# A MoBA chain woven through a projection: its load in three pieces, its output transposes moved off it, and its last slots run into the next product

## The chip, the cores and the metric

The kernel runs on one core of a Trainium2 chip. The metric is the device time of one execution in microseconds (us), the median of several runs.

## The reference

A first block and two layers of a second block run over 256 tokens of width 2048, all in float32. The change is in the first block and at one layer boundary of the second. What is computed there, cut to its core:

```
u = rmsnorm(x)
q_a, k_a, v_a, z_a, beta, dec, q_b, k_b, v_b, gate_a, gate_b = split(u @ w_in)
y_a = rmsnorm(delta_rule(conv(q_a, k_a, v_a), beta, dec)) * silu(z_a)      # 8 heads of 128
q_b, k_b = rmsnorm(q_b), rmsnorm(k_b)                                     # per head
y_b = softmax(q_b @ k_b.T * scale + rel_bias, causal) @ v_b               # MoBA: 256 tokens are one block
mix = sigmoid(gate_a) * (y_a @ w_branch_gdn) + sigmoid(gate_b) * (y_b @ w_branch_moba)
h = x + mix @ w_out
...
x2 = layer_norm(ALPHA * x1 + gate * (o @ a_w_out))                        # end of layer 0 of the second block
k, v = split((x2 * (1 + scale) + shift) @ kv_w)                           # first product of the next layer
```

## The kernel before

**Products.** Every large product is a list of bodies and units (`PLAN`). A unit is one 256x512 piece of a weight: SyncE loads it into a ring of `RING` = 4 buffers (`raw`), ScalarE casts it to its high part `w_hi`, VectorE subtracts to get the low part `w_lo` (`split` on both engines), and TensorE multiplies high by high, low by high and high by low: 12 matmuls a unit in `chunk`. The split in slot j is for unit j + 4, and it waits until TensorE has used unit j, so a unit's operands are ready up to three units ahead. Beside it VectorE does one step of a long vector product per slot (`gemv`: a 128x512 piece `gemv_w`, double-buffered, loaded by SyncE in the same queue as the weights). On VectorE and ScalarE a slot is: `between(j)`, then `split`, then (VectorE) `gemv`; on TensorE it is the unit's matmuls, then `due(j)`.

**The chain.** The product "spill" has 8 bodies of 16 units, so 128 slots, numbered here 0 to 127. It computes z, q_b, k_b, v_b and the gates and stores them to DRAM (`spill`). Through the same slots each engine steps a generator `delta_net`, one `next(mixer, None)` per slot, which runs the delta rule and then MoBA attention. The code between two `yield`s is the work of one slot; `rest(n)` is n empty slots; engines meet through semaphores. Slots 0 to 89 are the delta rule. From slot 90 on, before the change:

| | ScalarE | VectorE | TensorE |
|---|---|---|---|
| 90 | load all of `qkv_b` (3 MB), `o_sq` half 0 | | `rel_sum` |
| 91 to 94 | `o_sq` half 1, store `rel_scr`, `root_o`, load `bias_b` (1 MB) | `squares`, `over_root(0)` | |
| 95, 96 | 96: wait for `qkv_b`, `sq_b` half 0 | `gated(0)`, `over_root(1)`, `gated(1)` | |
| 97 | | `squares_b(0)` | transposes of `o_gdn`, pairs 0 and 1 (`ya_ready`) |
| 98 | `ya_high(0)`, `(1)`, `sq_b` half 1 | | pairs 2 and 3 (need `ya_low(0)`, `(1)`) |
| 99 | `ya_high(2)`, `(3)` | `ya_low(0)`, `(1)` | |
| 100 | | `ya_low(2)`, `(3)`, `squares_b(1)` | |
| 101 to 103 | `root_qkb` | norms of q_b and k_b (`qkb_normed`) | 103: first transposes of `qkv_b` |
| 107 on | | | scores of head 0, a head every two slots |

`turn_all` transposes a pair of blocks into one of two PSUM banks; a bank comes free (`turn_free`) when VectorE has taken the low part out of it. The last MoBA step is in slot 125 on TensorE, 126 on ScalarE and 127 on VectorE.

**The next product.** "branch" has 4 bodies of 8 units: four with `ya`, four with `yb`, each with its own gate. After slot 127 ScalarE stores the last spill piece, waits for `yb_done` and for all spill stores, and loads `gates` (two transfers, 4 MB) before its next `split`. `gates` lies over `qkv_b`.

**The layer tail.** At the end of "o2" (and "o3") VectorE's `body` calls `finish` in unit 14 of 16: it drains the last accumulators, adds the residual and takes statistics. Then it does the splits of slots 14 and 15 (they are units 2 and 3 of the next product "v3"), and only then come `bn_aggr`, the root, `normalized`, and the first operand blocks of v3 (`even_block`, `block_low` on VectorE, `odd_block` on ScalarE).

## Time and profile before

| | |
|---|---|
| time, median of 3 runs | 2687.71 us (2687.5 to 2688.08) |
| the profiled execution | 2689.27 us, of which span 2687.5 us |
| TensorE busy | 2616.5 us, 97% of the span |
| VectorE, ScalarE busy | 1820.6 us (68%), 1180.0 us (44%) |
| mean granted TensorE clock | 0.99 |
| bytes moved | 604.93 MB, mean 225 GB/s |

Matmuls are pipelined, so a matmul's row is longer (0.40 us) than the step from one to the next; where TensorE stands still shows as idle time before a row. All times below are microseconds from the start of the span.

### The profile page before, as it was taken

The page shows a single profiled execution, that of the slowest core. Times are in us where ns is not written, and L with a number is a line of the kernel's source. Part 1 is how long each engine was busy: PE and PEld are TensorE (multiplying, and loading weights), DVE is VectorE, ACT ScalarE, POOL GpSimd, SP SyncE. Part 2 cuts the span into 40 slices and gives each one's busy share as a digit, 9 for nine tenths or more (in the row PEclk, how much of TensorE's full clock was granted, in tenths as well). Part 3 has the DMA queues.
Part 4 walks back from the last instruction along what each step waited for, and adds up shares of the span by engine and source line. Part 5 has one row for each costly group of instructions (what it writes and reads, how often), then busy time and mean ns, then how long its engine had stood idle before and what let it go on. Part 6 is the DMA issues. An engine that isn't in the chain of part 4 may idle for free.

```text
span 2687.5 us, 37571 instructions
## 1 busy us (share of the span) xinstructions
PE 2616.5 (97%) x13990; PEld 2207.0 (82%) x13990; DVE 1820.6 (68%) x2371; ACT 1180.0 (44%) x1489; POOL 0.2 (0%) x4
## 2 busy tenths in 40 slices
PE   8999999989999999999999999999999989999997
PEld 8977878767788787888887888799987768999885
DVE  6788667576567777777776667776777665545655
ACT  4464333345434444444443334433386344334642
POOL 0000000000000000000000000000000000000000
PEclk9999999989999999999999999999999999999998
DMA  7677575676757788888887777888845546665463
GB/s 216 193 235 244 182 230 193 213 257 202 255 192 262 252 274 266 272 274 272 271 276 258 246 248 251 277 270 273 264 143 188 182 154 178 184 214 170 126 219 126
DMA packets 313000, 604.93 MB, mean 225 GB/s; under 512 B 26606, under 2 KB 28660, under 8 KB 310684
## 3 DMA queue, kind: packets, MB, share of 16 engines
q1 hardware_dynamic: 301628, 571.92, 66.6%
q10 hardware_dynamic: 11232, 31.10, 3.2%
q8 instruction: 94, 1.54, 0.2%
q14 instruction: 46, 0.38, 0.0%
HBM read 592.31 MB, written 10.62 MB: 224 GB/s over the span
## 4 chain that ended last, share of the span: by engine, by line
PE 90%; DVE 4%; DMA 2%; issue 2%; ACT 2%; DVEq 0%; ACTq 0%; SPq 0%
PE bank L613 21%; PE bank L615 21%; PE bank L614 21%; PE bank L636 6%; PE bank L638 6%; PE bank L637 6%; PE bank L733 2%; PE bank L575 2%; DMA gemv_w<-in_w_mod 1%; ACT w_hi L1215 1%; DVE w_lo L1808 1%; DVE gemv_acc L1833 1%; PE bank L1052 1%; DMA raw<-in_w_branch_gdn 0%; PE bank L941 0%
## 5 line engine op out<-in xcount | busy, mean ns | idle before, releaser
L1808 DVE TENSOR_TENSOR w_lo<-raw,w_hi 128x1024 fp32r<-128x1024 f32 x820 | 1001.7, 1224 | 795.0 <-ACT w_hi L1215 793.4
L1215 ACT CAST w_hi<-raw 128x1024 fp32r<-128x1024 f32 x820 | 860.2, 1050 | 1387.2 <-PE bank L615 1045.8
L613 PE MATMUL bank<-w_hi,u_hi 128*128 128x512 f32 x1216 | 494.8, 407 | 2.1 <-DVE u_lo L1869 2.1
L614 PE MATMUL bank<-w_lo,u_hi 128*128 128x512 f32 x1216 | 484.6, 398 | 0.0
L615 PE MATMUL bank<-w_hi,u_lo 128*128 128x512 f32 x1216 | 484.5, 398 | 0.0
L1833 DVE SCALAR_TENSOR_TENSOR gemv_acc<-gemv_w,small,gemv_acc 128x512 f32<-128x512 f32 x480 | 358.4, 747 | 21.6 <-DMA gemv_w<-in_w_mod 16.1
L613 PE MATMUL bank<-w_hi,s_hi 128*128 128x512 f32 x768 | 310.6, 404 | 1.2 <-DVE w_lo L1808 1.1
L615 PE MATMUL bank<-w_hi,s_lo 128*128 128x512 f32 x768 | 304.3, 396 | 0.0
L614 PE MATMUL bank<-w_lo,s_hi 128*128 128x512 f32 x768 | 304.1, 396 | 0.0
L636 PE MATMUL bank<-s_hi,w_hi 128*128 128x256 f32 x1024 | 289.5, 283 | 0.0
L637 PE MATMUL bank<-s_lo,w_hi 128*128 128x256 f32 x1024 | 288.3, 282 | 0.0
L638 PE MATMUL bank<-s_hi,w_lo 128*128 128x256 f32 x1024 | 288.3, 282 | 0.0
L613 PEld LDWEIGHTS bank<-w_hi,u_hi 128*128 128x128 f32 x1216 | 231.2, 190 | 62.0 <-issue 8.2
L615 PEld LDWEIGHTS bank<-w_hi,u_lo 128*128 128x128 f32 x1216 | 230.9, 190 | 56.5
L614 PEld LDWEIGHTS bank<-w_lo,u_hi 128*128 128x128 f32 x1216 | 231.5, 190 | 51.9
L637 PEld LDWEIGHTS bank<-s_lo,w_hi 128*128 128x128 f32 x1024 | 193.3, 189 | 0.3
L638 PEld LDWEIGHTS bank<-s_hi,w_lo 128*128 128x128 f32 x1024 | 193.2, 189 | 0.0
L636 PEld LDWEIGHTS bank<-s_hi,w_hi 128*128 128x128 f32 x1024 | 192.0, 187 | 0.7 <-issue 0.5
L615 PEld LDWEIGHTS bank<-w_hi,s_lo 128*128 128x128 f32 x768 | 144.7, 188 | 35.2
L613 PEld LDWEIGHTS bank<-w_hi,s_hi 128*128 128x128 f32 x768 | 144.7, 188 | 34.7 <-DVE w_lo L1808 1.5
L614 PEld LDWEIGHTS bank<-w_lo,s_hi 128*128 128x128 f32 x768 | 144.9, 189 | 32.6
L613 PE MATMUL bank<-w_hi,hid_hi 128*128 128x512 f32 x352 | 140.0, 398 | 0.0
(355 smaller groups left out, 3012.1 us busy)
## 6 DMA issues: line engine op xcount, KB each, us to landing
gemv_w<-in_w_mod SPq DMA_DIRECT2D x384, 256.0 KB, 3.1
raw<-in_w_in SPq DMA_DIRECT2D x176, 512.0 KB, 4.3
raw<-in_a_w_in SPq DMA_DIRECT2D x128, 512.0 KB, 4.5
raw<-in_w_ffn_gate SPq DMA_DIRECT2D x88, 512.0 KB, 4.6
raw<-in_w_ffn_up SPq DMA_DIRECT2D x88, 512.0 KB, 4.4
raw<-in_w_ffn_down SPq DMA_DIRECT2D x88, 512.0 KB, 4.1
gemv_w<-in_kv_w_mod SPq DMA_DIRECT2D x128, 256.0 KB, 3.6
raw<-in_kv_w SPq DMA_DIRECT2D x64, 512.0 KB, 3.7
```

The lines of the kernel that those rows point to most:

```text
L575: ins = pe.transpose(b[:, f * T + th * P:f * T + (th + 1) * P], src(f, th), ident)
L613: pe.matmul(o, xh, w_hi[:, s, t], start=(k == 0), stop=False)
L614: pe.matmul(o, xh, w_lo[:, s, t], start=False, stop=False)
L615: ins = pe.matmul(o, xl, w_hi[:, s, t], start=False, stop=(k == 2 * units - 1))
L636: pe.matmul(o, wh, hi[:, k], start=(k == 0 and f % 2 == 0), stop=False)
L637: pe.matmul(o, wh, lo[:, k], start=False, stop=False)
L638: ins = pe.matmul(o, wl, hi[:, k], start=False, stop=(k == 2 * half - 1 and f % 2 == 1))
L733: ins = pe.matmul(dst[:, h * P:(h + 1) * P], lhs[:, th, h], rhs[:, th, h], start=True, stop=True)
L1052: ins = pe.matmul(b[:, P:3 * P], queries_of[p][:, a, P:T], k_t[:, a, 0:T], start=True, stop=not mask)
L1215: act.copy(w_hi[:, s], raw[:, s]).then_inc(hi_done, 1)
L1808: dve.tensor_tensor(w_lo[:, s], raw[:, s], w_hi[:, s].bitcast(F32), ALU.subtract).then_inc(lo_done, 1)
L1833: dve.scalar_tensor_tensor(out=gemv_acc[:], in0=w_k, scalar=c_k, in1=gemv_acc[:], op0=ALU.mult, op1=ALU.add).then_inc(gemv_step, 1)
```

## The change

The chain is moved by some slots, its load is cut in three, and its last steps run on into the first body of "branch":

- **The load.** `qkv_b` comes in three transfers of 1 MB: q and k of half 0 in slot 90, of half 1 in slot 92 (ahead of the store of `rel_scr`), all of v in slot 99. The squares wait for the first two, `moba_out(0)` for the third.
- **The output transposes.** TensorE transposes `o_gdn` pairs 0 and 1 in slot 100 (before: 97) and 2 and 3 in slot 102 (before: 98). `ya_high` is in ScalarE's slots 101 and 103 (before: 98, 99), `ya_low` in VectorE's 101 and 104 (before: 99, 100). `squares_b(1)` is in slot 99 (before: 100), behind `sq_b` half 1 in ScalarE's slot 98. `root_qkb` stays in slot 101, the norms in 102 and 103.
- **Two slots later.** The transposes of `qkv_b` begin in TensorE's slot 105 (before: 103), the scores of head 0 in 109 (before: 107). The last steps are in slots 127 (TensorE), 128 (ScalarE) and 129 (VectorE), so the two latter in "branch".
- **The gates.** `gates` lies over `u_hi` and `u_lo`, which are dead after "spill", and ScalarE loads them in slot 1 of "branch", after one more split and without waiting for `yb_done`. `o_gdn`, `ya_lo`, `bias_b`, `mix_hi`, `mix_lo` and two of the delta rule's buffers move to other places.
- **The layer tail.** `finish` ends the body; the splits of slots 14 and 15 come behind `even_block(0)` and `block_low(0)`.

```diff
@@ placement @@
-        o_gdn = slot("o_gdn", 13, [P, H1, HALVES, DH])
+        o_gdn = slot("o_gdn", 10, [P, H1, HALVES, DH])
...
-        gates = slot("gates", 0, [P, HALVES, 2 * D])
-        mix_hi = slot("mix_hi", 4, [P, KD, T], F32R)
-        mix_lo = slot("mix_lo", 10, [P, KD, T], F32R)
+        gates = slot("gates", 3, [P, HALVES, 2 * D])
+        mix_hi = slot("mix_hi", 11, [P, KD, T], F32R)
+        mix_lo = slot("mix_lo", 13, [P, KD, T], F32R)
@@ TensorE: delta_net @@
-                yield from rest(7)
+                yield from rest(10)
                 n0 = products["branch"].ahead0
                 pe.wait_ge(signal("ya_ready"), HALVES)
                 for q in range(H1 // 2):
                     turn_all(n0 + q, 1, lambda f, th: o_gdn[:, 2 * q + f, th])
-                    if q % 2:
-                        yield
-                yield from rest(4)
+                    if q == 1:
+                        yield from rest(2)
+                yield from rest(3)
@@ ScalarE: delta_net @@
+                def qkvb_load(th, blocks):
+
+                    n = DH * blocks.start
+                    src = halves(spill[:, SPILL_QKV + n:SPILL_QKV + DH * blocks.stop])
+                    act.dma_start(qkv_b[:, th, blocks].rearrange("p h b c -> p h (b c)"), src[:, th]).then_inc(signal("qkvb_in"), 16)
+
+                first, values = slice(0, 2 * H1), slice(2 * H1, 3 * H1)
...
-                act.dma_start(qkv_b[:].rearrange("p h b c -> p h (b c)"), halves(spill[:, SPILL_QKV:SPILL_GATES])).then_inc(
-                    signal("qkvb_in"), 16)
+                qkvb_load(slice(0, 1), first)
...
+                qkvb_load(slice(1, 2), first)
                 act.wait_ge(signal("rel_ready"), 2)
                 act.dma_start(rel_scr, rel_rows[0:H1, :]).then_inc(signal("rel_out"), 16)
...
-                act.wait_ge(signal("qkvb_in"), 16)
+                act.wait_ge(signal("qkvb_in"), 32)
...
+                qkvb_load(slice(0, HALVES), values)
@@ ScalarE: behind "spill" @@
-            act.wait_ge(signal("yb_done"), H1)
-            act.wait_ge(signal("spilledA"), 16 * products["spill"].bodies)
-            act.wait_ge(signal("spilledB"), 16 * products["spill"].bodies)
-            for x in range(2):
-                act.dma_start(gates[:, :, x * D:(x + 1) * D], halves(spill[:, SPILL_GATES + x * D:SPILL_GATES + (x + 1) * D])).then_inc(
-                    signal("gates_in" + "AB"[x]), 16)
+            def first_branch(j):
+                if j == 1:
+                    act.wait_ge(signal("spilledA"), 16 * products["spill"].bodies)
+                    act.wait_ge(signal("spilledB"), 16 * products["spill"].bodies)
+                    for x in range(2):
+                        first = SPILL_GATES + x * D
+                        act.dma_start(gates[:, :, x * D:(x + 1) * D], halves(spill[:, first:first + D])).then_inc(
+                            signal("gates_in" + "AB"[x]), 16)
+                next(mixer, None)
...
@@ VectorE: body @@
-                    ending = finish and j == pr.units - 2
-                    if ending:
-                        gemv(pr, i, j)
+                    if finish and j == pr.units - 2:
                         finish()
+                        return
@@ VectorE: behind layer_tail("o2", ...) @@
             even_block(0)
+            split(o2, o2.bodies - 1, o2.units - 2)
             block_low(0)
+            split(o2, o2.bodies - 1, o2.units - 1)
```

Three places show how the order of instructions moves. The first is VectorE from slot 97 on; `small<-sq_b` is `squares_b`, and a `w_lo` row with the `gemv_acc` row behind it is the split and the vector step of one slot. Before:

```order
L2054 TENSOR_REDUCE small<-sq_b 128x16
L1808 TENSOR_TENSOR w_lo<-raw,w_hi 128x1024
L1833 SCALAR_TENSOR_TENSOR gemv_acc<-gemv_w,small,gemv_acc 128x512
L1808 TENSOR_TENSOR w_lo<-raw,w_hi 128x1024
L1833 SCALAR_TENSOR_TENSOR gemv_acc<-gemv_w,small,gemv_acc 128x512
L1865 TENSOR_TENSOR ya_lo<-bank,ya_hi 128x512 x2
L1808 TENSOR_TENSOR w_lo<-raw,w_hi 128x1024
L1833 SCALAR_TENSOR_TENSOR gemv_acc<-gemv_w,small,gemv_acc 128x512
L1865 TENSOR_TENSOR ya_lo<-bank,ya_hi 128x512 x2
L2054 TENSOR_REDUCE small<-sq_b 128x16
```

The same place in the changed kernel:

```order
L2071 TENSOR_REDUCE small<-sq_b 128x16
L1827 TENSOR_TENSOR w_lo<-raw,w_hi 128x1024
L1852 SCALAR_TENSOR_TENSOR gemv_acc<-gemv_w,small,gemv_acc 128x512
L1827 TENSOR_TENSOR w_lo<-raw,w_hi 128x1024
L1852 SCALAR_TENSOR_TENSOR gemv_acc<-gemv_w,small,gemv_acc 128x512
L1882 TENSOR_TENSOR ya_lo<-bank,ya_hi 128x512 x2
L1827 TENSOR_TENSOR w_lo<-raw,w_hi 128x1024
L1852 SCALAR_TENSOR_TENSOR gemv_acc<-gemv_w,small,gemv_acc 128x512
L2102 RECIPROCAL small<-small 128x32
L2105 TENSOR_TENSOR qkv_b<-qkv_b,small 128x2048
```

The second `squares_b` has moved one slot ahead of where it was, the first two `ya_low` two slots back; the other two now stand behind both norms (`qkv_b<-qkv_b,small`).

The second place is ScalarE where "spill" ends and "branch" begins: `stage<-bank` and `spill<-stage` are the last spill piece. Before, and then changed:

```order
L1463 CAST yb_hi<-bank 128x256
L1215 CAST w_hi<-raw 128x1024 x2
L1345 ACT_TABLE_LOAD
L1345 ACTIVATE stage<-bank 128x512 x2
L1347 DMA spill<-stage 128x2x512
L1540 DMA gates<-spill 128x2x2048 x2
L1215 CAST w_hi<-raw 128x1024 x8
```

```order
L1473 COPY probs_t<-bank 128x384
L1219 CAST w_hi<-raw 128x1024
L1349 ACT_TABLE_LOAD
L1349 ACTIVATE stage<-bank 128x512 x2
L1351 DMA spill<-stage 128x2x512
L1477 CAST yb_hi<-bank 128x256
L1219 CAST w_hi<-raw 128x1024
L1554 DMA gates<-spill 128x2x2048 x2
L1219 CAST w_hi<-raw 128x1024 x7
```

One cast of "branch" and the last `yb_hi` now stand between the last store and the load of the gates.

The third place is VectorE at the end of "o2", from the last statistics; `xs<-xs,small` is `normalized`, `stage<-bank,modc` is `even_block`, `s_lo` is `block_low`. Before, and then changed:

```order
L2443 BN_STATS small<-xs 128x6 x2
L1808 TENSOR_TENSOR w_lo<-raw,w_hi 128x1024 x2
L2474 BN_AGGR small<-small 128x2 x2
L2483 RECIPROCAL small<-small 128x2
L2498 TENSOR_SCALAR xs<-xs,small 128x512 x4
L2373 TENSOR_SCALAR stage<-bank,modc 128x256 x2
L2380 TENSOR_TENSOR s_lo<-stage,s_hi 128x512
L2373 TENSOR_SCALAR stage<-bank,modc 128x256 x2
L2380 TENSOR_TENSOR s_lo<-stage,s_hi 128x512
```

```order
L2464 BN_STATS small<-xs 128x6 x2
L2495 BN_AGGR small<-small 128x2 x2
L2504 RECIPROCAL small<-small 128x2
L2519 TENSOR_SCALAR xs<-xs,small 128x512 x4
L2394 TENSOR_SCALAR stage<-bank,modc 128x256 x2
L1827 TENSOR_TENSOR w_lo<-raw,w_hi 128x1024
L2401 TENSOR_TENSOR s_lo<-stage,s_hi 128x512
L1827 TENSOR_TENSOR w_lo<-raw,w_hi 128x1024
L2394 TENSOR_SCALAR stage<-bank,modc 128x256 x2
```

The two splits that stood ahead of `BN_AGGR` are now one ahead of the first `block_low` and one behind it.

## Rows read from the trace of the kernel before

**Rows 1.** The waits of TensorE, 540 to 740: total, times, longest.

```profile
PE bank L575 <- DVE o_gdn L2049: 7.6, 1, 7.6
PE bank L575 <- DVE qkv_b L2090: 5.0, 1, 5.0
PE bank L575 <- DVE ya_lo L1865: 3.7, 1, 3.7
PE bank L613 <- DVE w_lo L1808: 3.0, 2, 1.7
```

**Rows 2.** TensorE in time, 567 to 616: start, duration, instruction, idle before it.

```profile
575.07 1.97 PE L575 MATMUL bank<-keep,o_gdn 128*128 128x128 f32 x8 [7.57 <-DVE o_gdn L2049]
576.68 0.78 PE L613 MATMUL bank<-w_hi,u_hi 128*128 128x512 f32 x1
...
580.07 0.40 PE L615 MATMUL bank<-w_hi,u_lo 128*128 128x512 f32 x1
...
584.88 1.97 PE L575 MATMUL bank<-keep,o_gdn 128*128 128x128 f32 x8 [3.71 <-DVE ya_lo L1865]
...
607.87 1.97 PE L575 MATMUL bank<-keep,qkv_b 128*128 128x128 f32 x8 [4.98 <-DVE qkv_b L2090]
609.49 0.78 PE L613 MATMUL bank<-w_hi,u_hi 128*128 128x512 f32 x1
...
614.18 0.39 PE L615 MATMUL bank<-w_hi,u_lo 128*128 128x512 f32 x1
614.41 1.04 PE L575 MATMUL bank<-keep,qkv_b 128*128 128x128 f32 x8
615.20 0.48 PE L613 MATMUL bank<-w_hi,u_hi 128*128 128x512 f32 x1
```

**Rows 3.** Windows: length, busy PE, PEld, DVE, ACT, POOL, PEclk, DMA share, GB/s.

```profile
544.00:570.00 26.00, 23.50 (x100) 17.99 (x98) 17.14 (x20) 15.97 (x16) 0.00 (x0) 0.99 0.97 341
570.00:610.00 40.00, 26.24 (x99) 21.16 (x100) 30.81 (x31) 16.87 (x21) 0.00 (x0) 0.76 0.58 188
717.30:730.50 13.20, 11.48 (x49) 8.95 (x49) 5.85 (x7) 3.47 (x4) 0.00 (x0) 1.00 1.00 394
```

**Rows 4.** VectorE by line, 544 to 610: busy, mean ns, idle before.

```profile
L1808 DVE TENSOR_TENSOR w_lo<-raw,w_hi 128x1024 fp32r<-128x1024 f32 x15 | 18.3, 1221 | 12.2 <-ACT w_hi L1215 12.1
L1833 DVE SCALAR_TENSOR_TENSOR gemv_acc<-gemv_w,small,gemv_acc 128x512 f32<-128x512 f32 x14 | 10.5, 748 | 6.6 <-DMA gemv_w<-in_w_mod 6.6
L2054 DVE TENSOR_REDUCE small<-sq_b 128x16 f32<-128x2048 f32 x2 | 4.6, 2280 | 0.0
```

**Rows 5.** VectorE in time, slots 96 to 103.

```profile
573.79 1.22 DVE L2049 TENSOR_TENSOR o_gdn<-o_gdn,z_sb 128x1024 f32<-128x1024 f32 x1
...
584.15 1.28 DVE L1865 TENSOR_TENSOR ya_lo<-bank,ya_hi 128x512 fp32r<-128x512 f32 x2
...
605.53 2.29 DVE L2090 TENSOR_TENSOR qkv_b<-qkv_b,small 128x2048 f32<-128x2048 f32 x1
```

**Rows 6.** Transfers issued 540 to 620: size, time to landing.

```profile
gemv_w<-in_w_mod SPq DMA_DIRECT2D x17, 256.0 KB, 3.1
qkv_b<-spill ACTq DMA_DIRECT2D x1, 3072.0 KB, 13.5
bias_b<-rel_scr ACTq DMA_DIRECT2D x1, 1024.0 KB, 8.5
```

**Rows 7.** ScalarE in time where "branch" begins.

```profile
714.79 3.89 ACT L1215 CAST w_hi<-raw 128x1024 fp32r<-128x1024 f32 x4 [6.50 <-issue]
...
728.14 2.23 ACT L1215 CAST w_hi<-raw 128x1024 fp32r<-128x1024 f32 x2 [9.46 <-DMA raw<-in_w_branch_gdn]
```

**Rows 8.** VectorE in time at the end of "o2".

```profile
2154.95 2.35 DVE L1808 TENSOR_TENSOR w_lo<-raw,w_hi 128x1024 fp32r<-128x1024 f32 x2
...
2162.93 0.69 DVE L2380 TENSOR_TENSOR s_lo<-stage,s_hi 128x512 fp32r<-128x512 f32 x1 [1.42 <-ACT s_hi L1619]
```

**Rows 9.** TensorE in time at the end of "o2".

```profile
2159.39 0.88 PE L575 MATMUL bank<-keep,xs 128*128 128x128 f32 x3 [8.21 <-issue]
```

More of the change, by code:

```diff
@@ L193, in block_kernel @@
         ya_hi = slot("ya_hi", 7, [P, H1, T], F32R)
[L194 removed]
+        ya_lo = slot("ya_lo", 10, [P, H1, T], F32R)
         qkv_b = slot("qkv_b", 0, [P, HALVES, 3 * H1, DH])
@@ L198, in block_kernel @@
         qk_t = slot("qk_t", 8, [P, 2 * H1, T])
-        bias_b = slot("bias_b", 10, [P, H1, T])
+        bias_b = slot("bias_b", 13, [P, H1, T])
         rel_rows = slot("rel_rows", 11, [P, 512])
@@ L951, in _ @@
                 plain_body("spill", i, u_hi, u_lo, due)
-            for _ in mixer:
-                pass
             pr = products["branch"]
@@ L962, in due @@
                 def due(j):
-                    if j == 1 and not (isinstance(i, int) and i == 0):
+                    if isinstance(i, int) and i == 0:
+                        next(mixer, None)
+                    elif j == 1:
                         turn_mixed(i - 1)
@@ L967, in branch_body @@
                 if isinstance(i, int) and i == 0:
+                    for _ in mixer:
+                        pass
                     pe.wait_ge(signal("yb_done"), H1)
@@ L1408, in delta_net @@
                 yield from rest(2)
-                act.wait_ge(signal("qkvb_in"), 16)
+                act.wait_ge(signal("qkvb_in"), 32)
                 act.activation(sq_b[:], qkv_b[:, 0, 0:2 * H1], ACT.Square).then_inc(signal("qkb_sq"), 1)
+                yield from rest(2)
+                act.wait_ge(signal("qkb_ss"), 1)
+                act.activation(sq_b[:], qkv_b[:, 1, 0:2 * H1], ACT.Square).then_inc(signal("qkb_sq"), 1)
+                yield
+                qkvb_load(slice(0, HALVES), values)
                 yield from rest(2)
@@ L1545, in mixed_high @@
                     his_of_stage(products["branch"], i, 0, mix_hi)
-            body("branch", 0, nothing)
+            body("branch", 0, nothing, first_branch)
             with act.Fori(1, pr.bodies) as i:
@@ L2078, in delta_net @@
                 yield from rest(2)
+                squares_b(1)
+                yield from rest(2)
                 ya_low(0)
@@ L2081, in delta_net @@
                 yield
-                ya_low(2)
-                ya_low(3)
-                squares_b(1)
-                yield from rest(2)
                 dve.wait_ge(signal("root_qkb"), 1)
@@ L2092, in delta_net @@
                     yield
-                yield from rest(4)
+                ya_low(2)
+                ya_low(3)
+                yield from rest(6)
                 for at_ in range(1, B_LAST + 7):
@@ L2266, in _, with first_branch @@
                 body("spill", i, nothing, between)
-            for _ in mixer:
-                pass
             pr = products["branch"]
+            def first_branch(j):
+                next(mixer, None)
+                if j == 4:
+                    for _ in mixer:
+                        pass
             def branch_drain(pr, i, x):
@@ L2285, in mixed_low @@
                     los_of_stage(products["branch"], i, 0, mix_lo, mix_hi)
-            body("branch", 0, branch_drain)
+            body("branch", 0, branch_drain, first_branch)
             with dve.Fori(1, pr.bodies - 1) as i:
```

33 lines of the change are left out of this document (17 added, 16 removed).

## Prediction

> **What bounds the kernel now.** TensorE is busy 97% of the span, so a change pays only where TensorE stands still. The view of who waited for whom, cut to TensorE and to the stretch of the change, comes first [rows 1]: three single waits of its transposes, 7.6, 5.0 and 3.7 us, all for VectorE, and two waits of matmuls for `w_lo`, 3.0 us together, the longer 1.7. The timeline of TensorE places the first three [rows 2]: A at 575.07 (slot 97, for `ya_ready`), B at 584.88 (slot 98, for the bank that `ya_low(0)` frees), C at 607.87 (slot 103, for the norms). The reader is to see there also what follows each: the 8 transposes of A take 576.68 - 575.07 = 1.61 us, the same 8 at 614.41 take 0.79. The windows [rows 3] say why: the granted clock is a mean of 0.76 over 570 to 610, after 0.99 before, so TensorE runs part of it at the lower of its two levels. Last comes VectorE in the same stretch [rows 4, 5]: it is late because it is loaded and because its vector step waits 6.6 us for `gemv_w`, while the transfers run at a share of 0.97 [rows 3], with 3 MB of `qkv_b` and 1 MB of `bias_b` among them [rows 6].
>
> **What the three waits cost.** Idle: 7.57 + 3.71 + 4.98 = 16.3 us [rows 2]. Slow clock after A: 1.61 - 0.79 = 0.8 on the transposes, and the 8 matmuls from 576.68 to 580.07 take 3.39 instead of 8 x 0.235 = 1.88 (0.235 is the step at full clock; one shows from 614.18 to 614.41), 1.5 more: 2.3. B's transposes have the same row of 1.97 as A's, so B gets 2.3 too. After C, 1.62 - 0.79 = 0.8, and 11 matmuls from 609.49 to 614.18 take 4.69 instead of 2.6: 2.9. Together 7.5. The whole is 16.3 + 7.5 = 23.8 us.
>
> **What is left of it.** A: `gated(1)` ended at 575.01 [rows 5], but now TensorE wants it three slots later, after unit 100: 3 x 2.82 = 8.5 us of cover (12 matmuls of 0.235 are 2.82) against 7.57. Even with all of VectorE's old lag it is hidden; if the cover were gone it would cost the 7.57 and the clock. B was built in: bank 0 was wanted straight after slot 98, and `ya_low(0)` stood in VectorE's slot 99, behind a cast and a split. Now it stands in slot 101 and is wanted after unit 102. Is it in time? In the trace of before `gated(1)` ends 7.57 after unit 97, and 6.6 of these are VectorE's waits for `gemv_w` [rows 4]; without them it would be 1.0. From there to the end of `ya_low(0)` VectorE has 5 splits and 5 vector steps (5 x (1.22 + 0.75) = 9.9), two `squares_b` (2 x 2.28 = 4.6) and half a `ya_low` row (0.64) [rows 4, 5], and about 1.5 of waiting, since `sq_b` is one buffer: ScalarE's second square waits for the first sum, and the cast stands behind it. That is 16.6, or 15.6 with neighbouring rows overlapping by some 0.08 each. TensorE takes 5 x 2.82 plus 2 x 0.79 for transposes = 15.7. So `ya_low(0)` is late by 1.0 + 15.6 to 16.6 - 15.7 = 0.9 to 1.9 (I take 1.0, since neighbouring rows do overlap), plus what is left of the `gemv_w` waits. C: the norms and the second pair of `ya_low` come in slots 102 to 104 (2 x 2.29 + 1.28 + 3 splits and steps, 5.9, = 11.8), wanted after unit 105 (3 x 2.82 + 2 x 0.79 = 10.0, counted from the transposes of slot 102): near 1 us of wait for the bank of `ya_low(2)`, since VectorE is nearer its limit than TensorE here.
>
> **The load in pieces.** Nothing shows this load cut, so its effect on `gemv_w` is bounded from both sides. Below: none of the 6.6 us is left, since `gemv_w` is ahead by about one slot and lands in 3.1 when undisturbed [rows 6]. Above: all 6.6. Before slot 97 the bytes beside the weights fall from 4 to 3 MB (v waits until slot 99), which by proportion leaves 5.0; but the old 3 MB stood in one block of 13.5 us, and now 1 MB stands alone, two slots pass, and the next comes. I take 2.5. A rule speaks against the change here. The Trainium skill, "DMA: Bandwidth & Descriptors", section "Issuing engines are not separate DMA queues", says that transfers issued by SP and ACT run on the same 16 engines and interleave whoever started them, so cutting a transfer moves its bytes and removes none; by it all 6.6 us would stay and the time be that of the first rival below, 2671.7, against 2665.3 by the value taken. No row of this trace shows the cut load.
>
> The new waits are then 1.0 + 2.5 at slot 102 and 1.0 at slot 105: **4.5 us** (ends: 0 and 1.9 + 6.6 + 1.0 + 2.3 of clock = 11.8). The chain gives 23.8 - 4.5 = **19.3 us**. The attention slots themselves are only shifted by two; their small waits stay.
>
> **The start of "branch".** Before, ScalarE stood from the last store to its landing and then did four casts in a row from 714.79 [rows 7]; the first of them fed the first `yb` unit, which TensorE awaited for 3.0 - 1.7 = 1.3 us [rows 1]. One cast is now ahead of that wait: 1.3 gained. The next wait, 1.7, is behind the gates: transfers at a share of 1.00 and 394 GB/s [rows 3], ScalarE 9.46 us without a weight [rows 7]. One weight load is now issued ahead of the gates, the rest still queue with them: 0 to 1.7 gained, I take 0.7. The last chain steps on ScalarE and VectorE (slots 128, 129) are hidden under four `ya` units, 11.3 us; without that cover they cost a slot each. Sum **2.0**. The new places of the buffers cost nothing: the same instructions run on the same shapes.
>
> **The layer tail.** Two splits, 2.35 us, leave the path from the statistics to the first transposes of v3, where TensorE stands 8.21 us [rows 8, 9]. The first goes into the 1.42 us that VectorE waited ahead of `block_low(0)` [rows 8] and is free; the second delays `even_block(2)` by 1.2 and what hangs on it. Gain 2.35 - 1.2 = **1.1** (0 to 2.35). At "o3" no split stood there, so nothing.
>
> **Sum.** 19.3 + 2.0 + 1.1 = 22.4. The profiled execution took 2689.27 (span 2687.5), 1.56 above the median of the runs: 2689.3 - 22.4 = 2666.9, and 2687.7 - 22.4 = **2665.3** as a median.
>
> **Rivals.**
> 1. *The lag stays.* The pieces disturb `gemv_w` as the whole did, VectorE is 1.0 + 6.6 = 7.6 late at slot 102, a wait of that length brings the slow clock, 2.3, and 1.0 follows. Waits 10.9, chain gain 12.9, total 16.0: 2671.7. For it: the DMA share of 0.97. Against: a megabyte less in that stretch.
> 2. *All hidden.* No new waits, 1.7 all gone, the tail gives 2.35: 23.8 + 3.0 + 2.35 = 29.2: 2658.5.
> 3. *The change doesn't do what it says.* VectorE is the bound, and TensorE waits as long, only elsewhere: it ends the norms when it did. Then only "branch" and the tail pay: 3.1, so 2684.6, no change that can be told. Against: VectorE was idle 9.2 us of 570 to 610 [rows 3], mostly for casts that themselves stood behind TensorE's waits.
> 4. *The other side.* TensorE's waits were when the transfers caught up; without them the ring of weights starves. The 17 slots from 544 to 614 need 17 x 0.786 MB of weights and vectors (768 KB each) plus 5.2 MB: 18.6 MB. At the 341 GB/s of 544 to 570 [rows 3] that is 54 us, as long as TensorE needs without any wait, against 70 us now. It costs more than the change brings only below 18.6 / 70 = 266 GB/s. If the rate under mixed queues fell to 225, the mean of the kernel (in the table of the profile), it is 83 us, 13 more: 13 - 3 = 10 slower, 2698.
>
> **Chances.** Forecast 0.60 (2661 to 2669), rival 1 0.22, rival 2 0.10, rival 3 0.05, rival 4 0.03. The range takes in rivals 1 and 2 and the ends of the new waits: 2657 to 2675. What a measurement can tell from no change is about 0.2%, 5.4 us: faster 0.92, same 0.05, slower 0.03.
>
> **What would show it.** In the profile after: no wait of TensorE on `o_gdn` at slot 100; one of about 3.5 us on `ya_low(0)` at slot 102; about 1 at the first transposes of `qkv_b`; the granted clock near 1 over the stretch; VectorE's wait for `gemv_w` at 2 to 3 us instead of 6.6; the first `w_lo` wait of "branch" gone; 5.9 instead of 8.2 us ahead of v3's transposes, about 1 of it given back in v3's first units. The prediction is wrong if the wait at slot 102 is over 7, if matmuls begin to wait for `w_lo` between slots 97 and 107, or if the gates push a longer wait into the second body of "branch".

## The result and the profile after

| | before | after |
|---|---|---|
| median | 2687.61 us (2686.59 to 2689.44, 6 runs) | 2669.45 us (2666.77 to 2672.71, 6 runs) |
| profiled execution | 2689.27 us, span 2687.5 | 2669.09 us, span 2667.3 |

The ratio is 0.9932, 95% interval [0.9921, 0.9942]: 18.2 us faster by the medians, 20.2 by the two profiled executions. The forecast was 2665.3 (22.4 us gained), the range 2657 to 2675.

First the view of who waited for whom, TensorE, 540 to 740, of the changed kernel (the answer to [rows 1]):

```profile
PE bank L575 <- DVE ya_lo L1882: 4.8, 2, 4.1
PE bank L575 <- DVE stage L2301: 2.1, 1, 2.1
```

The wait for `o_gdn` and the one for the norms are gone, and so are both for `w_lo`. Of 19.3 us in these rows before, 6.9 are left. 2.1 of them are a wait on `stage` (the product with the gates), which before was 0.7 and is not in the rows shown. TensorE in time (start, duration, instruction, idle before it), for [rows 2]:

```profile
575.37 1.04 PE L575 MATMUL bank<-keep,o_gdn 128*128 128x128 f32 x8
...
586.67 1.97 PE L575 MATMUL bank<-keep,o_gdn 128*128 128x128 f32 x8 [4.15 <-DVE ya_lo L1882]
588.29 0.78 PE L613 MATMUL bank<-w_hi,u_hi 128*128 128x512 f32 x1
588.86 0.63 PE L614 MATMUL bank<-w_lo,u_hi 128*128 128x512 f32 x1
589.29 0.46 PE L615 MATMUL bank<-w_hi,u_lo 128*128 128x512 f32 x1
589.59 0.39 PE L613 MATMUL bank<-w_hi,u_hi 128*128 128x512 f32 x1
...
598.14 1.16 PE L575 MATMUL bank<-keep,qkv_b 128*128 128x128 f32 x8 [0.66 <-DVE ya_lo L1882]
```

The first pair of output transposes (slot 100) finds its data and runs at full clock: 1.04 us. The second (slot 102) waits 4.15 us for the bank, and behind the wait comes the low clock again: 1.97 for the same work, and some 0.6 us more until the matmuls are back at 0.39. The windows (columns as in [rows 3]) say the same of the whole stretch; the last is the branch product up to `mix_hi`:

```profile
544.00:570.00 26.00, 26.00 (x112) 20.33 (x111) 21.12 (x24) 16.76 (x17) 0.00 (x0) 1.00 0.95 329
570.00:610.00 40.00, 35.19 (x169) 28.24 (x168) 34.49 (x35) 22.88 (x29) 0.00 (x0) 0.96 0.85 285
686.50:781.60 95.10, 92.97 (x412) 74.79 (x411) 56.82 (x62) 38.26 (x42) 0.00 (x0) 1.00 0.65 225
```

Over 570 to 610 the granted clock is 0.96 instead of 0.76, TensorE is busy 35 us instead of 26, and the transfers, which stood at 188 GB/s, run at 285. VectorE is now busy for 34.5 of 40 us. Its waits for `gemv_w` (by line, 544 to 610, as in [rows 4]) and the transfers issued (as in [rows 6]):

```profile
L1852 DVE SCALAR_TENSOR_TENSOR gemv_acc<-gemv_w,small,gemv_acc 128x512 f32<-128x512 f32 x18 | 13.5, 748 | 3.1 <-DMA gemv_w<-in_w_mod 3.0
```

```profile
gemv_w<-in_w_mod SPq DMA_DIRECT2D x22, 256.0 KB, 3.5
qkv_b<-spill ACTq DMA_DIRECT2D x3, 1024.0 KB, 7.7
bias_b<-rel_scr ACTq DMA_DIRECT2D x1, 1024.0 KB, 10.6
```

**Where the 20.2 us came from.** Three instructions of TensorE mark the stretches in every kernel: the `rel_sum` product of the chain, the first matmul with `ya_hi`, and the first with `mix_hi`. Before, they start at 547.03, 704.58 and 801.55; after, at 546.58, 686.50 and 781.54. The chain gave 157.55 - 139.92 = 17.6 us, the branch product 96.97 - 95.04 = 1.9. With 0.45 won ahead of the change, that is 20.0 of 20.2. The layer tail gave the rest:

```profile
2137.24 1.94 PE L575 MATMUL bank<-keep,xs 128*128 128x128 f32 x8 [6.07 <-issue]
2139.51 1.94 PE L575 MATMUL bank<-keep,xs 128*128 128x128 f32 x8 [0.33 <-DVE stage L2394]
...
2146.41 1.03 PE L575 MATMUL bank<-keep,xs 128*128 128x128 f32 x8
```

The wait ahead of v3's transposes fell from 8.21 [rows 9] to 6.07. But unit 0 of v3 and what hangs on it then took longer, and by the transposes ahead of unit 1 only 0.2 us of it is left in this execution. Other executions of the same instructions keep more (experiment 4).

### The profile page after: what moved, and what is told of

Its sections match the earlier page's. It is cut to its first block, busy times and chain, and to the rows that moved or that the text cites. A ratio compares the mean times of both kernels' runs of the same rounds, so it can differ in the third digit from the quotient of the medians.

```text
span 2667.3 us, 37574 instructions
## 1 busy us (share of the span) xinstructions
PE 2611.7 (98%) x13990; PEld 2203.6 (83%) x13990; DVE 1820.8 (68%) x2371; ACT 1179.5 (44%) x1489; POOL 0.2 (0%) x4
## 4 chain that ended last, share of the span: by engine, by line
PE 91%; DVE 4%; issue 2%; ACT 2%; DMA 2%; DVEq 0%; ACTq 0%; SPq 0%
PE bank L613 21%; PE bank L615 21%; PE bank L614 21%; PE bank L636 6%; PE bank L638 6%; PE bank L637 6%; PE bank L733 2%; PE bank L575 1%; DVE w_lo L1827 1%; ACT w_hi L1219 1%; DVE gemv_acc L1852 1%; DMA gemv_w<-in_w_mod 1%; PE bank L1056 1%; DMA raw<-in_w_branch_gdn 0%; PE bank L943 0%
```

## Experiments

The runs of one kernel scatter by 2 to 5 us around its median, and several questions here are of 1 us. So each kernel was timed in 5 runs (`pieces_only` in 11) beside the kernel before, and its profiled execution read by the same three marks. "Chain" is `rel_sum` to `ya_hi`, "branch" `ya_hi` to `mix_hi`; slot 102 and 105 are the waits ahead of the second output transposes and of the first of `qkv_b` (in turn_later slot 103 and 105, in turn_shift 103 and 106, in the kernels with the order before 97, 98 and 103).

| kernel | median (before beside it) | ratio | chain | branch | waits of the transposes |
|---|---|---|---|---|---|
| before | 2687.61 | | 157.55 | 96.97 | 7.57, 3.71, 4.98 |
| changed | 2669.45 (2687.61) | 0.9932 [0.9921, 0.9942] | 139.92 | 95.04 | 4.15, 0.66 |
| one_load | 2669.97 (2686.04) | 0.9941 [0.9927, 0.9954] | 142.31 | 93.96 | 3.71, 0.24 |
| pieces_only | 2683.18 (2686.04) | 0.9990 [0.9981, 0.9999] | 153.18 | 97.34 | 3.92, 3.71, 4.97 |
| branch_undone | 2668.66 (2686.04) | 0.9935 [0.9921, 0.9948] | 140.23 | 94.19 | 3.73, 0 |
| tail_undone | 2668.38 (2686.04) | 0.9933 [0.9919, 0.9946] | 140.55 | 96.51 | 3.72, 0 |
| second_sq | 2666.72 (2687.12) | 0.9930 [0.9916, 0.9944] | 139.07 | 96.34 | 3.19, 0.35 |
| turn_later | 2669.25 (2687.12) | 0.9941 [0.9927, 0.9954] | 139.94 | 94.55 | 0, 4.60 |
| turn_shift | 2671.18 (2687.12) | 0.9942 [0.9929, 0.9956] | 142.75 | 95.38 | 1.21, 1.78 |
| warm_tail | 2666.45 (2687.12) | 0.9929 [0.9915, 0.9942] | 140.21 | 94.55 | 3.71, 0 |
| gates_split | 2666.47 (2687.02) | 0.9922 [0.9908, 0.9935] | 139.28 | 93.35 | 3.54, 0.51 |
| bias_late | 2666.68 (2687.02) | 0.9924 [0.9910, 0.9937] | 137.75 | 94.60 | 2.06, 1.78 |
| best3 | 2664.05 (2687.02) | 0.9915 [0.9901, 0.9929] | 138.93 | 93.64 | 3.12, 0.50 |
| best4 | 2663.91 (2687.02) | 0.9913 [0.9899, 0.9927] | 138.30 | 93.24 | 2.62, 0.24 |

How far to trust one execution can be read there too: five kernels have the changed chain untouched (changed, branch_undone, tail_undone, warm_tail, gates_split), and their chains lie between 139.3 and 140.6. Seven have its branch product untouched (changed, one_load, tail_undone, second_sq, turn_later, warm_tail, bias_late): 94.0 to 96.5, mean 95.1. A single execution inside these bands shows no difference.

What makes these bands can be read too. In every kernel with the order of the changed one whose clock stays at 1.00 there, the branch stretch is 92.9 plus TensorE's waits in it: 95.04 with 2.13 of them, 96.34 with 3.49 (second_sq), 93.96 with 1.10 (one_load). In tail_undone (96.51) the clock was at 0.50 from 718.3 to 721.7 besides, and so it was in pieces_only (97.34) from 717.1 to 720.5. The profiled execution of pieces_only is its slowest of 11, 3.9 us above their median.

### 1 and 2. All but the load, and the load alone

`one_load` is the changed kernel with the whole 3 MB issued where the first piece stood:

```diff
-                    pe.wait_ge(signal("qkvb_in"), 3 * 16)
+                    pe.wait_ge(signal("qkvb_in"), 16)
...
-                qkvb_load(slice(0, 1), first)
+                act.dma_start(qkv_b[:].rearrange("p h b c -> p h (b c)"), halves(spill[:, SPILL_QKV:SPILL_GATES])).then_inc(
+                    signal("qkvb_in"), 16)
...
-                qkvb_load(slice(1, 2), first)
...
-                act.wait_ge(signal("qkvb_in"), 32)
+                act.wait_ge(signal("qkvb_in"), 16)
...
-                qkvb_load(slice(0, HALVES), values)
```

> The changed kernel with one load of 3 MB at slot 90 in place of three pieces; everything else as changed. If the large load is what made VectorE wait for gemv_w (my step 2), the waits of gemv between slots 92 and 97 go back from 3.3 to about 6 us, gated(1) ends 3 us later against the rel_sum product, and the transposes of o_gdn at slot 100 wait 1 to 3 us, with the one at slot 102 as long or longer: 2 to 4 us slower than the changed kernel, near 2672. Rival (the pieces do nothing, the other transfers of that stretch are what VectorE waits for): gemv waits stay within 1 us of 3.3, time within 1 us of 2669.

`pieces_only` is the kernel before with these edits the other way round and nothing else.

> The kernel before with only the load cut in three pieces; transposes where they were. My step 2 says that VectorE is 2.5 to 3.3 us earlier at gated(1), and the wait of the transposes at slot 97 falls from 7.57 to 4.3 to 5; the waits at slots 98 and 103 hang on ScalarE and VectorE inside the chain and keep most of their 3.71 and 4.98: 2684 to 2685, a sixth of the whole gain. Rival (the three waits share one cause, the load): all three shrink and the time falls by 8 us or more, to 2680 or below.

VectorE by line, 544 to 610, in one_load and then in pieces_only:

```profile
L1851 DVE SCALAR_TENSOR_TENSOR gemv_acc<-gemv_w,small,gemv_acc 128x512 f32<-128x512 f32 x17 | 12.7, 745 | 6.1 <-DMA gemv_w<-in_w_mod 6.1
```

```profile
L1843 DVE SCALAR_TENSOR_TENSOR gemv_acc<-gemv_w,small,gemv_acc 128x512 f32<-128x512 f32 x15 | 11.2, 747 | 2.9 <-DMA gemv_w<-in_w_mod 2.9
```

The wait for `gemv_w` follows the shape of the load in both orders: 6.6 and 6.1 with one block, 2.9 and 3.1 with pieces, and 1.9 to 4.9 in all twelve executions with pieces. The first rival of the prediction is out. The pieces are smaller, further apart, and the last one is later; which of the three does it was not tested apart. VectorE's lag follows: `gated(1)` starts 26.8 and 26.3 us after `rel_sum` with the block, 23.1 and 23.5 with pieces. In one_load TensorE doesn't wait at slot 100 either, against what was expected; the lag shows as 2.3 us of waits for `w_lo` ahead of it, and the chain is 2.4 us longer, outside the band. The times of one_load and the changed kernel alone can't be told apart. In pieces_only only the wait at slot 97 shrinks, from 7.57 to 3.92:

```profile
PE bank L575 <- DVE qkv_b L2100: 5.0, 1, 5.0
PE bank L575 <- DVE o_gdn L2059: 3.9, 1, 3.9
PE bank L575 <- DVE ya_lo L1875: 3.7, 1, 3.7
```

The others hang on the order inside the chain, as expected. So the pieces are worth 2.4 us (behind the moved transposes) to 4.4 us (in front of them) of chain, 2.9 by the medians; the moves of transposes, squares and norms are worth the other 13 to 15.

### 3. The start of the branch product as before

Chain drained ahead of the branch product on all three engines, gates loaded only after `yb_done`; here ScalarE's part:

```diff
-            def first_branch(j):
-                if j == 1:
...
-            body("branch", 0, nothing, first_branch)
+            for _ in mixer:
+                pass
+            act.wait_ge(signal("yb_done"), H1)
...
+            body("branch", 0, nothing)
...
```

> The changed kernel with the branch product started as before: the chain drained ahead of it on all three engines, the gates loaded only after yb_done. My step 3 prices that at 2.0 us: the stretch from the first matmul with ya_hi to the first with mix_hi goes from 95.0 back to about 97.0, and the waits at its start (1.3 for the first w_lo, 0.7 more) come back: 2671.5. Rival (the wait of 2.13 us on the stage that now stands in body 1 shows that the work is only moved): within 0.5 us of the changed kernel.

The stretch did not go back to 97: it took 94.2, inside the band of the changed one. The waits were 0.5 (`w_lo`) and 0.6 (`stage`), where the changed kernel has one of 2.1. Running on into the next product is worth nothing that shows here. What TensorE waits for in this place begins in ScalarE's row of transfers. In the changed kernel:

```profile
689.02 0.37 ACTq L1351 DMA_DIRECT2D spill<-stage  x1
689.42 0.37 ACT L1477 CAST yb_hi<-bank 128x256 fp32r<-128x256 f32 x1 [0.44 <-ACT stage L1349]
689.69 1.06 ACT L1219 CAST w_hi<-raw 128x1024 fp32r<-128x1024 f32 x1
694.99 0.89 ACTq L1554 DMA_DIRECT2D gates<-spill  x2
```

and of VectorE there:

```profile
702.57 1.29 DVE L2296 TENSOR_TENSOR stage<-bank,gates 128x512 f32<-128x512 f32 x2 [2.02 <-DMA gates<-spill]
```

ScalarE stands from 690.75 to 694.99 until the last store has landed; the gates leave 5.97 us after it was issued. Their first half, the one that VectorE needs, lands 7.5 us later, the second 13.9, and VectorE waits 2.0. From the issue of the store to that of the gates, 3.95 to 5.97 us pass from execution to execution (before 5.48, branch_undone 3.95).

An early store does not help by itself. In one_load, turn_later, warm_tail, bias_late and tail_undone the gates leave 2 us earlier against the first `ya_hi` matmul than in the changed kernel, 6.5 for 8.5, and the first half lands no earlier: 15.7 to 16.9 for 16.0. In branch_undone the gates also leave at 6.5, but the first half lands at 13.8, after 7.4 us instead of 9.3 to 10.3. There no cast stands ahead of them. With the new order the cast frees a buffer, and one 512 KB weight load goes out at 5.7, ahead of the gates; the changed kernel's gates, which left 2.8 us behind that load and not 0.7 to 1.8, took 7.5 again. That this load is what delays the gates is argued from these times, not shown by a run of its own. So the order seems to have two effects here: the wait for `w_lo` of 0.5 goes, and the one on `stage` grows from 0.6 to between 1.1 and 3.5.

### 4. The layer tail as before

The two last splits of o2 go back ahead of the layer norm.

```diff
-            split(o2, o2.bodies - 1, o2.units - 2)
             block_low(0)
-            split(o2, o2.bodies - 1, o2.units - 1)
...
```

> The changed kernel with the end of the attention layer as before (both last splits of o2 ahead of the layer norm). By my step (1.1 us net) the first unit of the second v3 body would come 1.1 us later. By the rival read from the trace of the changed kernel (the 2.1 us won ahead of v3's transposes are lost again because TensorE keeps its lower clock to the end of the first v3 unit): transposes of xs 2.1 us later, but the transposes of unit 1 only 0 to 0.4 us later, and the first unit takes 2.9 us again instead of 4.8. In the whole time no more than 0.4 us, below what the timing can tell.

From VectorE's first row behind o2 (`stage<-bank,gate_bc`; 2151.22 before, 2131.21 changed, 2132.95 here), TensorE's transposes of `xs` start 8.17, 6.03 and 8.16 us later, those ahead of unit 1 15.39, 15.20 and 15.38 later. In these profiles the edit wins 2.1 us and keeps 0.2. The windows from the first transposes to those ahead of unit 1 show why; the kernel before, then the changed one:

```profile
2159.39:2166.60 7.21, 6.75 (x28) 5.34 (x29) 5.48 (x11) 4.05 (x8) 0.00 (x0) 0.70 0.18 67
```

```profile
2137.24:2146.40 9.16, 8.70 (x28) 6.82 (x29) 7.79 (x13) 4.21 (x8) 0.00 (x0) 0.53 0.40 114
```

The same 28 matmul rows took 7.2 us at a mean clock of 0.70 and 9.2 at 0.53: TensorE began earlier and ran almost all of it at the lower level.

But the 0.2 is of these executions. Three kernels have the tail as before and eight the changed one, with nothing added to it. Microseconds behind VectorE's first row behind o2:

| tail | kernel | clock back at 1.00 | transposes ahead of unit 1 |
|---|---|---|---|
| as before | before, tail_undone, pieces_only | 12.4, 12.1, 11.9 | 15.39, 15.38, 15.37 |
| changed | bias_late, branch_undone | 11.5, 11.5 | 13.86, 13.87 |
| changed | second_sq, turn_later | 12.3, 12.6 | 14.15, 14.26 |
| changed | one_load, changed, turn_shift, gates_split | 14.6, 14.7, 14.7, 14.9 | 15.16, 15.20, 15.23, 15.27 |

The first transposes come at 6.0 in all eight, so that 2.1 us are always won; what is left of them goes with the moment at which the clock comes back. In four executions it is 0.1 to 0.2 us, in four 1.1 to 1.5, and 0.75 on the mean. The window of bias_late beside the two above (7.84 us at a mean clock of 0.65):

```profile
2135.87:2143.71 7.84, 7.38 (x28) 5.60 (x28) 7.24 (x13) 3.58 (x7) 0.00 (x0) 0.65 0.38 96
```

### 5. A buffer of its own for the second squares

```diff
-                act.wait_ge(signal("qkb_ss"), 1)
-                act.activation(sq_b[:], qkv_b[:, 1, 0:2 * H1], ACT.Square).then_inc(signal("qkb_sq"), 1)
+                act.activation(sq_b1[:], qkv_b[:, 1, 0:2 * H1], ACT.Square).then_inc(signal("qkb_sq"), 1)
...
-                    dve.tensor_reduce(sm(MX + th * 2 * H1, 2 * H1), sq_b[:], AX.X, ALU.add).then_inc(signal("qkb_ss"), 1)
+                    dve.tensor_reduce(sm(MX + th * 2 * H1, 2 * H1), (sq_b, sq_b1)[th][:], AX.X, ALU.add).then_inc(signal("qkb_ss"), 1)
```

> The changed kernel with a buffer of its own for the squares of the second token half (over the dead o_sq), so that ScalarE no longer waits 4.70 us for VectorE's sum of the first half. Theory (VectorE's own queue sets the 4.15 us wait at slot 102; from gated(1) to ya_low(0) it is idle only 1.12 + 0.34 us, and the 1.12 is ScalarE's late cast): the 1.12 goes, the wait at slot 102 falls to about 3.0, 1 us faster than the changed kernel. Rival (ScalarE's 4.70 wait is what is late): the wait at slot 102 falls below 1 us, 4 us faster or more.

The wait at slot 102 is 3.19 for 4.15, and the chain 139.07 for 139.92, 0.2 below the band. The other executions with this place untouched had 3.5 to 3.7 there, so that a ScalarE wait of 4.70 us taken away gives TensorE 0.5 to 0.9. ScalarE was not what was late.

### 6 and 7. The second transposes a slot later, alone and with all that follows

```diff
                     if q == 1:
-                        yield from rest(2)
-                yield from rest(3)
+                        yield from rest(3)
+                yield from rest(2)
...
                 ya_high(0)
                 ya_high(1)
-                yield from rest(2)
+                yield from rest(3)
                 ya_high(2)
                 ya_high(3)
-                yield from rest(3)
+                yield from rest(2)
```

The first part is TensorE's, the second ScalarE's: `ya_high(2)` and `(3)` move with the transposes.

> The changed kernel with the second pair of output transposes one slot later (103 in place of 102), the transposes of qkv_b where they were. If VectorE's queue is the bound between slots 97 and 105, the wait only moves: about 1.3 us at slot 103 and about 3 at slot 105, the stretch from rel_sum to ya within 1 us of 139.9, less the clock that a shorter wait keeps. Rival (the wait at 102 is one of latency alone): 1.3 at slot 103, the 0.66 at slot 105 unchanged, 3 us faster.

TensorE in turn_later:

```profile
585.10 1.25 PE L575 MATMUL bank<-keep,o_gdn 128*128 128x128 f32 x8
...
596.57 1.62 PE L575 MATMUL bank<-keep,qkv_b 128*128 128x128 f32 x8 [4.60 <-DVE ya_lo L1882]
```

4.15 + 0.66 = 4.81 of waits became 4.60, three slots on, and the chain is 139.94 after 139.92. So VectorE's queue bounds this stretch, with what it waits for itself: TensorE gets there no earlier wherever it waits. Between the end of `gated(1)` and the start of `ya_low(0)` VectorE stands idle for 1.5 of 14.7 us in the changed kernel.

In turn_shift the second rest stays 3, on all three engines, so that all behind it comes a slot later.

> The changed kernel with the second pair of output transposes and all of the chain behind it one slot later on all three engines. If VectorE is behind by a fixed amount there, one more unit of TensorE (2.8 us) covers most of the 4.15 wait at slot 102: 1.3 us left, no lower clock behind it (0.9 us more), and the chain, which ended 5.8 us ahead of the first yb_hi product, still ends 3 us ahead of it: 3 to 4 us faster than the changed kernel, near 2666. Rival (what ends the chain sets the start of the branch product): the wait moves to the first product with yb_hi, no gain.

The waits fell as expected (1.21 and 1.78, no low clock behind them), and the kernel got no faster: by the medians 1.7 us slower, which the timing can't tell; in the profile the chain is 2.8 us longer, and `yb_hi` wanted 14.0 us after `ya_hi` instead of 11.3. Two things went wrong. The exponentials of two heads now stand behind ScalarE's drain at the end of a body (two copies and a store), so that the waits for `probs` grew from 0.9 to 5.1 us (2.00 and 3.10), and with them came the low clock: 0.50 from 622.9 to 626.2 and from 657.0 to 663.8. ScalarE in turn_shift at one of the two:

```profile
617.69 1.07 ACT L1349 ACTIVATE stage<-bank 128x512 f32<-128x512 f32 x2
618.79 0.37 ACTq L1351 DMA_DIRECT2D spill<-stage  x1
619.19 1.28 ACT L1465 ACT_TABLE_LOAD   x1 [0.43 <-ACT stage L1349]
620.49 0.37 ACT L1465 ACTIVATE probs<-bank,small 128x128 f32<-128x128 f32 x1
```

And the end of the chain met the wait for the gates. ScalarE there:

```profile
692.33 0.37 ACTq L1351 DMA_DIRECT2D spill<-stage  x1
692.79 0.48 ACT L1473 COPY probs_t<-bank 128x384 f32<-128x384 f32 x1 [0.49 <-ACT stage L1349]
693.16 1.05 ACT L1219 CAST w_hi<-raw 128x1024 fp32r<-128x1024 f32 x1
696.33 1.11 ACTq L1554 DMA_DIRECT2D gates<-spill  x2
697.48 0.37 ACT L1477 CAST yb_hi<-bank 128x256 fp32r<-128x256 f32 x1 [3.27 <-issue]
```

The last `yb_hi` cast stood 3.27 us behind a wait for a store that has nothing to do with it. The changed kernel has that cast one slot ahead of the wait, at 689.42.

### 8. TensorE kept busy across the layer norm

```diff
+            for _ in range(36):
+                pe.transpose(bank[OUTS][:, 0:P], ident, ident)
             turn_normed(0)
```

> The changed kernel with 36 transposes of the identity into an unused bank behind the last product of o2, so that TensorE does not stand still before v3's first transposes; they add work and no result. If the gain of the earlier split is lost to the lower clock of the first v3 unit, the transposes of xs take 1.04 us in place of 1.94 each and the unit 2.9 in place of 4.84: up to 3 us faster by the position of the second unit's transposes, unless VectorE (scaling and low parts of the blocks) takes over the wait, then 1 us. Rival (the clock does not answer to such transposes): clock 0.5 and 4.84 us as before, same time.

The transposes ahead of unit 1 come 13.10 us after VectorE's first row behind o2 instead of 15.20 in the changed kernel's profile and 13.9 to 15.3 in the eight of experiment 4: 0.8 to 2.2 us won, 1.5 on their mean. With 48 transposes (in best3) there is no low clock at all, and it is 13.08. The windows say what is left; warm_tail, then best3:

```profile
2135.79:2142.90 7.11, 6.29 (x29) 5.09 (x29) 7.11 (x13) 3.58 (x7) 0.00 (x0) 0.76 0.37 93
```

```profile
2131.86:2138.90 7.04, 5.20 (x28) 3.89 (x28) 7.04 (x13) 3.52 (x7) 0.00 (x0) 1.00 0.37 87
```

Clock 0.76 or 1.00, the same 7.1 us: VectorE is busy for all of it in both. So this is all that a TensorE at full clock can give here, and it shows where the tail's gain had gone.

### 9. The two gate loads apart

```diff
-                if j == 1:
-                    act.wait_ge(signal("spilledA"), 16 * products["spill"].bodies)
+                if j in (0, 3):
+                    x = j // 3
+                    landed = products["spill"].bodies if x else products["spill"].bodies - 2
+                    act.wait_ge(signal("spilledA"), 16 * landed)
...
```

> The changed kernel with the two gate loads apart: the first half at the first slot of the branch product, waiting only for the spill writes two bodies back (its columns landed long ago), the second half three slots later, behind the last write. Theory (ScalarE stands 4 to 6 us behind the landing of the last spill write, and the 2.1 us wait of body 1 is VectorE's wait for the gates, both from the place of the load, not from the chain): gates issued about 5 us earlier, VectorE's wait of 2.02 gone, the stretch from the first ya_hi product to the first mix_hi product 93.2 to 94 us in place of 95.0. Rival (the waits come from the weights behind the 4 MB of gates): ScalarE's waits for raw stay at 7.5 and the stretch stays at 95.

```profile
689.61 0.37 ACTq L1351 DMA_DIRECT2D spill<-stage  x1
690.07 0.43 ACTq L1555 DMA_DIRECT2D gates<-spill  x1
695.93 0.37 ACTq L1555 DMA_DIRECT2D gates<-spill  x1
```

```profile
701.12 1.29 DVE L2297 TENSOR_TENSOR stage<-bank,gates 128x512 f32<-128x512 f32 x2 [0.15 <-DMA gates<-spill]
```

The first half now leaves 0.46 us after the store instead of 5.97, VectorE's wait is 0.15, TensorE's wait on `stage` 0.5, and the stretch 93.35. The three kernels with the gates apart (this one, best3, best4) have a mean of 93.4, all below the band of the seven others with its mean of 95.1: 1.7 us. ScalarE still waits for weights (7.50 in the changed kernel, 5.33 and 2.15 here), and it costs TensorE nothing. What the edit does is seen against the first `ya_hi` matmul:

| kernel | gates leave | first half lands | TensorE's waits in the stretch |
|---|---|---|---|
| before | 9.2 | 16.6 | 3.70 |
| changed | 8.5 | 16.0 | 2.13 |
| one_load | 6.5 | 15.7 | 1.10 |
| warm_tail | 6.5 | 16.4 | 1.68 |
| turn_later | 6.5 | 16.4 | 1.68 |
| bias_late | 6.5 | 16.4 | 1.75 |
| tail_undone | 6.6 | 16.9 | 2.09 |
| second_sq | 7.5 | 17.8 | 3.49 |
| branch_undone | 6.5 | 13.8 | 1.07 |
| gates_split, best3, best4 | 3.0 | 14.0, 14.2, 13.8 | 0.48, 0.77, 0.38 |

turn_shift and pieces_only are not in it: the wait in the former is the one of 1.79 for the chain's end, and the latter's stretch has the low clock in it.

So what holds this place up is the landing of the first 2 MB of the gates, which VectorE can use from about 14 on in the order of the changed kernel (16 in the one before). The edit brings it there by two things at once: the half leaves 3.5 us or more earlier, and it doesn't share the way with the other half. Which of the two does it was not tested. An issue 2 us earlier with both halves together did not (changed against warm_tail).

### 10. The bias load later

> The changed kernel with the 1 MB bias_b load moved from slot 94 to slot 99 and the values of qkv_b from 99 to 103. Theory (after the cut into pieces the transfers of slots 94 to 97 still hold gemv_w up): the gemv waits behind 558 go from 1.3 to below 0.5 us, and with VectorE bound through slot 102 the wait there falls by as much; 1 us faster in the stretch from rel_sum to ya. Rival: the two loads then collide with the weights at slots 99 to 105 and raise the wait ahead of the scores: no gain or 1 us slower.

The edit moves the load of `bias_b` from slot 94 to 99 and the values of `qkv_b` from 99 to 103. VectorE waited 1.9 us for `gemv_w` over 540 to 620, where it had been 3.0, and TensorE's waits became 2.06 and 1.78. After 2.06 the transposes took 1.25 us and the next matmul 0.48: no low clock. Chain 137.75, 2.2 shorter, below the band. About 1.5 of the 2.2 is the low clock that did not come in this execution. On top of the other edits (best4 beside best3) the chain was 0.6 shorter, inside the band, and VectorE waited 3.3 us for `gemv_w` in best4 and 3.2 in best3, so that the cause given for it is not borne out there. Whether the edit helps stays open.

### 11 and 12. Together

> The changed kernel with three edits together: squares of the second half in a buffer of their own, gate loads apart as above, and 48 transposes of the identity behind the last product of o2. By the stretches measured one by one (0.9 for the squares, 1 to 2 for the gates, 2 for the warm TensorE) 4 to 5 us faster than the changed kernel: 2664 to 2665. Rival (the gains share a wait): 2 us or less.

> The same three edits and the bias load at slot 99: by the theory for the bias another 1 us, by its rival nothing or 1 us lost against the three edits.

best3 ran in 2664.05 and best4 in 2663.91, 5.5 us under the changed kernel's median and 23 under the kernel before. Against the changed kernel's ratio the intervals still overlap (0.9913 [0.9899, 0.9927] and 0.9932 [0.9921, 0.9942]), so the time alone doesn't show it. By the three stretches best4 is 1.6 + 1.8 + 2.1 = 5.5 shorter than the changed kernel's profile, and about 1.7 + 1.8 + 1.5 = 5 shorter than the means of the untouched stretches. Bias or not can't be told between these two.

## Why the prediction was right, step by step

The profiled executions differ by 20.2 where 22.4 were forecast: chain 17.6 for 19.3, branch 1.9 for 2.0, tail 0.2 for 1.1, and 0.45 that lies ahead of the change and is scatter. The medians differ by 2.0 less, since before's profiled execution lay 1.66 above the median of its runs and the changed one's 0.36 below. The forecast had taken off 1.56 for the first and could not know the second.

- **The three waits and the slow clock, 23.8.** Right. What is left of both stands in the rows above, and the clock over 570 to 610 rose from 0.76 to 0.96.
- **The load in pieces, 6.6 to 2.5.** Right in mechanism; it came to 3.0. The Trainium skill, "DMA: Bandwidth & Descriptors", section "Issuing engines are not separate DMA queues", was weighed against it. The transfers here do share the engines, as it says: the share stayed at 0.95 and `bias_b` took 10.6 us instead of 8.5. But from shared engines it doesn't follow that nothing is gained; that step was mine. The same bytes cost `gemv_w` half the wait once they were spread (one_load, pieces_only).
- **New waits, 1.0 + 2.5 at slot 102 and 1.0 at 105, 4.5 together.** They came to 4.15 + 0.66 = 4.8. That VectorE's queue bounds the stretch was shown by turn_later (the wait moved and kept its size) and second_sq (4.7 us off ScalarE, 0.5 to 0.9 off TensorE).
- **The step that was mis-sized in the chain**: I gave the new wait at slot 102 no slow clock, though B's 3.71 us had cost 2.3 in my own sum. It cost 0.9 on the transposes and 0.6 or so behind them. With 0.3 more of waits that is about the 1.7 missing.
- **"One cast is now ahead of that wait: 1.3 gained", and 0.7 on the next wait.** This step failed, though its sum of 2.0 met the profile's 1.9; that it did is luck. With the old order back (branch_undone) the wait of 1.33 for the first `w_lo` was gone too, and the stretch as short (94.2): the store left 1.2 us earlier against the first `ya_hi` matmul and landed in 3.85 us instead of 5.39, so it was not the cast that took the wait away. And the weight load ahead of the gates gained nothing on the next wait: in the five kernels in which the gates leave at the same moment as in branch_undone, with that load ahead of them, they took 2 to 3 us longer. The change turned two waits for `w_lo` (1.33 and 1.70) and one of 0.67 on `stage` into one of 2.13 on `stage`, in the second body of "branch". That is one of my own signs of a wrong prediction, a longer wait pushed there by the gates, and it came true.
- **The layer tail, 2.35 - 1.2 = 1.1.** The split in the shadow of ScalarE and the delay of `even_block(2)` came as described, and 2.1 us were won ahead of the transposes. What I left out is the clock: TensorE, started 2.1 us sooner, took 1.9 us longer for the same rows, almost all of them at the lower level (tail_undone, warm_tail). Measured 0.2 in this profile. In the eight executions of the same tail it was 0.1 to 0.2 in four and 1.1 to 1.5 in the others, so that the size of 1.1 is inside what the edit gives and the 0.2 is an unlucky case. The 1.2 that I took off for `even_block(2)` can't be read apart from the clock.
- **Rivals.** Rival 1 fell with `gemv_w`. Rival 2 asked for no new waits and for none on the gates; there are 4.8 and 2.1 us. Rival 3 had a true core, since VectorE bounds slots 97 to 105, but it was the bound there only after TensorE's own waits were gone. Rival 4: no matmul of this stretch waits for `w_lo`, and the transfers went at 285 GB/s over 570 to 610, above the 266 it needed.

## What to carry to other kernels

When a wait is removed, ask which queue delivers the next one, and test it by moving the consumer one slot: if the wait keeps its size, that queue is the bound, and the only gain is to take work or waits off it. A gain ahead of a stretch that starts at the low clock is not a gain until the clock is back; price it at the next point behind the recovery, in more than one execution (here the same instructions kept 0.1 or 1.5 of 2.1 us), and fill the gap if there is nothing better to do. And follow a large load to the moment at which its first half is needed: 2 us sooner with both halves together brought nothing here, while the first half ahead of a store that it doesn't depend on, and apart from the second, did. A small load let out just ahead of it seems to have cost more than it brought.
